# The gate product, the projection of p and the final norm with tokens as rows

## What is computed

```python
h = h + moe(rms_norm(h, norm2_g))           # top-4 of 32 experts, 12 MB of weights each
h = h + sigmoid(rms_norm(h, norm3_g) @ w_ple_gate) * (p @ w_ple_proj)
y = rms_norm(h, final_g)                    # w_ple_gate 1024x1024, w_ple_proj 256x1024
```

## Time and profile before

| | |
|---|---|
| median of three runs | 1280.57 us |
| the profiled execution: its time, its span | 1280.34 us, 1278.6 us |
| busy: PE, PEld, DVE, ACT | 1232.8, 675.9, 357.7, 225.9 us |
| loaded and stored | 455.84 MB, mean 357 GB/s |

### The profile page before, as it was taken

One profiled execution on the slowest core, in us unless ns is written; L12 is line 12 of the kernel. 1 busy time (PEld: TensorE's weight loads), 2 busy tenths in 40 slices (PEclk: granted clock), 3 DMA queues, 4 the chain that ended last, 5 costly groups with the idle time before them and its releaser, 6 DMA issues.

```text
span 1278.6 us, 15794 instructions
## 1 busy us (share of the span) xinstructions
PE 1232.8 (96%) x6210; PEld 675.9 (53%) x6210; DVE 357.7 (28%) x960; ACT 225.9 (18%) x432; POOL 22.6 (2%) x51
## 2 busy tenths in 40 slices
PE   8999999999999999999999999999999999999988
PEld 6886778886435434344443444444344443434446
DVE  3423633226222212122221212312122221212136
ACT  2322322013111111111111011111111111111123
POOL 2000110000000000000000000000000000000000
PEclk9999999999999999999999999999999999999999
DMA  9642586844899999999999999999999999999970
GB/s 295 211 132 67 174 272 225 334 165 173 345 429 427 427 427 429 429 429 428 430 427 429 427 427 423 429 427 427 428 429 429 428 429 429 428 429 428 427 280 34
DMA packets 71060, 455.84 MB, mean 357 GB/s; under 512 B 6622, under 2 KB 40972, under 8 KB 46436
## 3 DMA queue, kind: packets, MB, share of 16 engines
q1 hardware_dynamic: 65328, 443.83, 84.5%
q0 software_dynamic: 2608, 9.08, 2.1%
q10 hardware_dynamic: 3076, 2.27, 0.6%
HBM read 449.33 MB, written 5.83 MB: 356 GB/s over the span
## 4 chain that ended last, share of the span: by engine, by line
PE 76%; DMA 20%; DVE 3%; ACT 1%; issue 1%; POOL 0%; SPq 0%; DVEq 0%; ACTq 0%
PE bank L879 38%; PE bank L638 17%; DMA ring<-in_w_up_dram 13%; PE bank L895 5%; DMA ring<-in_w_gate_dram 5%; PE bank L914 4%; PE bank L939 3%; PE bank L1135 2%; PE bank L887 2%; DMA out_dram<-ring 1%; DMA ring<-in_w_in_dram 1%; DVE regC L1596 1%; DVE regC L1578 1%; PE bank L902 0%; PE bank L680 0%
## 5 line engine op out<-in xcount | busy, mean ns | idle before, releaser
L879 PE MATMUL bank<-ring,regC 128*64 128x512 f32 x2080 | 461.0, 597 | 21.4 <-DVE regC L1596 13.3
L879 PEld LDWEIGHTS bank<-ring,regC 128*64 128x64 f32 x2080 | 145.3, 137 | 298.7 <-issue 270.0
L1578 DVE TENSOR_TENSOR regC<-bank,biasT 128x512 f32<-128x512 f32 x62 | 42.9, 692 | 597.6 <-PE bank L887 596.1
L879 PE MATMUL bank<-ring,xe_odd 128*64 128x512 f32 x896 | 198.7, 594 | 7.7 <-DMA ring<-in_w_up_dram 6.6
L638 PE MATMUL bank<-regA,ring 128*128 128x264 f32 x832 | 194.3, 390 | 0.0
L638 PEld LDWEIGHTS bank<-regA,ring 128*128 128x128 f32 x832 | 156.4, 191 | 31.4 <-issue 3.8
L879 PEld LDWEIGHTS bank<-ring,xe_odd 128*64 128x64 f32 x896 | 62.8, 137 | 131.7 <-issue 116.8
L895 PEld LDWEIGHTS bank<-regC,regB 128*128 128x128 f32 x816 | 96.0, 192 | 13.8 <-issue 12.8
L895 PE MATMUL bank<-regC,regB 128*128 128x128 f32 x816 | 100.6, 277 | 0.3 <-ACT regE L1969 0.3
L2017 ACT ACTIVATE regD<-bank 128x512 f32<-128x512 f32 x62 | 37.0, 597 | 243.5 <-PE bank L879 243.5
L1603 DVE TENSOR_TENSOR hT<-hT,bank 128x264 f32<-128x264 f32 x144 | 56.8, 425 | 81.0 <-PE bank L914 28.0
(11 more groups left out here) (342 smaller groups left out, 665.9 us busy)
## 6 DMA issues: line engine op xcount, KB each, us to landing
ring<-in_w_up_dram SPq DMA_DIRECT2D x64, 2048.0 KB, 26.6
ring<-in_w_down_dram SPq DMA_DIRECT2D x64, 2048.0 KB, 28.4
ring<-in_w_gate_dram SPq DMA_DIRECT2D x64, 2048.0 KB, 23.5
ring<-in_w_in_dram SPq DMA_DIRECT2D x28, 1024.0 KB, 6.1
out_dram<-ring POOLq DMA_DIRECT2D x9, 512.0 KB, 5.1
ring<-in_state_gla_dram POOLq DMA_DIRECT2D x8, 512.0 KB, 5.1
ring<-in_w_o_dram SPq DMA_DIRECT2D x4, 1024.0 KB, 7.5
ring<-in_w_ple_gate_dram SPq DMA_DIRECT2D x2, 2048.0 KB, 34.6
```

The costliest lines, as they stand in the source:

```text
L879: ins = mm(bank[b][n * CAP:(n + 1) * CAP, :], lhs(k + i), by_k[s][:, i, n * 512:(n + 1) * 512], start=(k + i == 0), stop=(k + i == KT - 1))
L1578: return v.tensor_tensor(out, v_in, bias.to_broadcast([P, HALF, 2, CAP]), ALU.add)
```

## The change

The last stage works with tokens as rows. The 128 tokens of a block, as columns of `n3T`, stay in the array and 512 columns of W_ple_gate stream past: `gate_step(b, n)` for two blocks and two halves. The samples' gate is made on four column groups: the result has its 1024 features as 4 groups of 8 rows by 256 columns. h is turned to rows and stays in PSUM, from which ScalarE squares it (the accumulator gives the sums over features) and VectorE adds it. The reciprocal root goes into the sigmoid as its scale, one number for each row. The projection of p is made as rows too, in 7 units instead of 8 tiles: four for the tokens (512 columns for each block, then 384), one for columns 512 to 639 of both blocks, and two for the samples. final_g is loaded anew as rows, by five DMAs. At the end there are two stores for the tokens and four for the samples.

The diff shows the new lines of the parts named, and what is replaced only where it is short; bookkeeping of buffers and the last scaling are left out.

```diff
-        pwT = view(regE, 0, KT, T)
-        SWT = [view(regE, KT * T + i * T, T) for i in range(2)]
+        pw, pw_s = view(regE, 0, NB, D), view(regE, NB * D, 2 * P)
+        SWT = [view(regE, NB * D + 2 * P + i * T, T) for i in range(2)]
         logitsT = SWT[1]
...
+        gated, gated_s = view(regC, 0, NB, D), view(regC, NB * D, 2 * P)
+        fgrow, fgrow_s = view(regD, D, D), view(regD, 0, 2 * P)
...
-        ROUTER_BANK, ROW_BANKS, PW_BANKS = 3, ((4, 5), (6, 7), (0, 1)), (2, 4, 5, 6, 7, 2, 4, 5)
+        ROUTER_BANK, ROW_BANKS, PW_BANKS = 3, ((4, 5), (6, 7), (0, 1)), (2, 7, 4, 6, 2, 4, 5)
...
-        PW_EARLY, PW_RANKED = 3, 5
+        PW_TOKENS = {0: (0, slice(0, 512)), 2: (1, slice(0, 512)), 4: (0, slice(IN_GAP * P, D)), 5: (1, slice(IN_GAP * P, D))}
+        PW_SAMPLE = {1: ((0, 2, 4), (1, 3)), 6: ((6,), (5, 7))}
+        PW_EARLY, PW_RANKED, PW_UNITS = 2, 4, 7
...
-        GATE_BANKS, YROW_BANKS = (3, 0, 1, 2), ((4, 6), (7, 3), (0, 1))
+        GATE_BANKS, H2_BANKS, S_BANK, H2_SUM_BANK, Y_SUM_BANK = ((3, 0), (4, 3)), ((5, 6), (1, 2)), 7, 4, 0
+        S_HALVES = (slice(0, 2 * P), slice(2 * P, 4 * P))
...
-            sp.wait_ge(pw_done, IN_GAP)
+            sp.wait_ge(pw_done, PW_RANKED)
...
+            sp.wait_ge(h2_ready, KT)
+            sp.dma_start(fgrow, final_g.unsqueeze(0).to_broadcast([P, D])).then_inc(ld_final, 16)
+            for q in range(4):
+                sp.dma_start(fgrow_s[q * E:(q + 1) * E, :],
+                             final_g[q * 2 * P:(q + 1) * 2 * P].unsqueeze(0).to_broadcast([E, 2 * P])).then_inc(ld_final, 16)
+
+            for b, rows, t0 in BLOCKS[:NB]:
                 sp.wait_ge(yrow_ready["vector"], b + 1)
                 sp.wait_ge(yrow_ready["scalar"], b + 1)
-                dst = y_prompt[0, t0:t0 + rows, :] if b < NB else y_sample[:, 0, :]
-                sp.dma_start(dst, x2[0:rows, b, :]).then_inc(y_stored, 16)
-            sp.wait_ge(y_stored, 16 * len(BLOCKS))
+                sp.dma_start(y_prompt[0, t0:t0 + rows, :], x2[0:rows, b, :]).then_inc(y_stored, 16)
+            sp.wait_ge(yrow_ready["vector"], NB + 1)
+            for q in range(4):
+                sp.dma_start(y_sample[:, 0, q * 2 * P:(q + 1) * 2 * P], x2[q * E:q * E + NS, NB, 0:2 * P])\
+                    .then_inc(y_stored, 16)
+            sp.wait_ge(y_stored, 16 * (NB + 4))
...
+            def pw_rows(out, b, cols):
+                rows, t0 = BLOCKS[b][1:]
+                for k in range(PK):
+                    ins = mm(out, pTv[:, k, t0:t0 + rows], proj_cols(k, cols), start=(k == 0), stop=(k == PK - 1))
+                return ins
+
+            def pw_unit(n):
+
+                ps = bank[PW_BANKS[n]]
                 for b in range(NB):
-                    if PW_BANKS[f] in ROW_BANKS[b]:
+                    if PW_BANKS[n] in ROW_BANKS[b]:
                         pe.wait_ge(x2_ready, b + 1)
-                if PW_BANKS[f] in PW_BANKS[:f]:
-                    pe.wait_ge(pw_ready, PW_BANKS.index(PW_BANKS[f]) + 1)
-                for k in range(PK):
-                    w, at = (proj, f * P) if f < IN_GAP else (proj_rest, (f - IN_GAP) * P)
-                    ins = mm(bank[PW_BANKS[f]][:, 0:T], w[:, k, at:at + P], pTv[:, k, :],
-                             start=(k == 0), stop=(k == PK - 1))
+                if n in PW_TOKENS:
+                    b, cols = PW_TOKENS[n]
+                    ins = pw_rows(ps[:, 0:cols.stop - cols.start], b, cols)
+                elif n in PW_SAMPLE:
+                    for k, f in [(k, f) for blocks in PW_SAMPLE[n] for k in range(PK) for f in blocks]:
+                        q, at = f // 2, 2 * P + f % 2 * P
+                        ins = mm(ps[q * E:q * E + NS, at:at + P], pTv[:, k, L:T], proj_cols(k, slice(f * P, (f + 1) * P)),
+                                 start=(k == 0), stop=(k == PK - 1), skip_group_check=True)
+                else:
+                    for b in range(NB):
+                        ins = pw_rows(ps[:, b * P:(b + 1) * P], b, slice(512, IN_GAP * P))
                 ins.then_inc(pw_done, 1)
...
-            pe.wait_ge(pw_ready, PW_BANKS.index(GATHER_BANK) + 1)
...
-            pe.wait_ge(pw_ready, PW_BANKS.index(GATHER_BANK + 1) + 1)
+            pe.wait_ge(pw_ready, PW_RANKED)
...
+            in_quarters = [2 * q + j for j in range(2) for q in range(4)]
+            def gate_step(b, n):
+                s, t0 = (LAST + n) % SLOTS, BLOCKS[b][2]
                 for k in range(KT):
+                    if (b, n) == (0, 0):
                         pe.wait_ge(h2_ready, k + 1)
+                    if (b, n) == (0, 1) and k == HALF:
+                        sample_sums(H2_SUM_BANK, h2_squares, 1, h2_ss).then_inc(h2_s_sum, 1)
                     kf = LAST_ADDED[k]
+                    ins = mm(bank[GATE_BANKS[b][n]][:, :], n3T[:, kf, t0:t0 + P], by_col[s][:, kf, :],
                              start=(k == 0), stop=(k == KT - 1))
                 ins.then_inc(gate_done, 1)
 
+            def sample_sums(at, squares, count, ss):
+                pe.wait_ge(squares, count)
+                for q in range(4):
+                    ins = mm(bank[at][q * E:(q + 1) * E, 0:1], of_group[:, :], ss[:, 4:5], start=True, stop=True)
                 return ins
 
+            pe.wait_ge(slot_loaded[LAST % SLOTS], expert_loads(LAST))
+            gate_step(0, 0)
+            pe.wait_ge(s_clear, 1)
+            for f in in_quarters:
+                q, at = f // 2, 2 * P + f % 2 * P
+                ins = mm(bank[S_BANK][q * E:q * E + NS, at:at + P], hTv[:, f, L:T], ident[:, :], start=True, stop=True)
+            ins.then_inc(h2_turned, 1)
+            for b, rows, t0 in BLOCKS[:NB]:
+                for n in range(2):
+                    for j in range(HALF):
+                        ins = turn(bank[H2_BANKS[b][n]][:, j * P:(j + 1) * P], hTv[:, n * HALF + j, t0:t0 + P], ident[:, :])
+                    ins.then_inc(h2_turned, 1)
+            pe.wait_ge(slot_loaded[(LAST + 1) % SLOTS], expert_loads(LAST + 1))
+            gate_step(0, 1)
+            for k in range(KT):
+                for q in range(4):
+                    ins = mm(bank[S_BANK][q * E:q * E + NS, S_HALVES[0]], n3T[:, k, L:T],
+                             by_col[(LAST + q // 2) % SLOTS][:, k, S_HALVES[q % 2]], start=(k == 0), stop=(k == KT - 1),
+                             skip_group_check=True)
+            ins.then_inc(gate_done, 1)
+            pe.wait_ge(h2_sum, 1)
+            gate_step(1, 0)
+            pe.wait_ge(gate_act, 1)
+            gate_step(1, 1)
+            pe.wait_ge(gate_act, 2)
+            sample_sums(Y_SUM_BANK, y_squares, 3, y_ss).then_inc(y_s_sum, 1)
...
+            dve.wait_ge(extra.added, n_extra * KT + KT)
+            v.memset(bank[S_BANK][:, :], 0.0).then_inc(s_clear, 1)
+            dve.wait_ge(h2_s_sum, 1)
+            v.tensor_scalar(h2_rs[:, NB:NB + 1], bank[H2_SUM_BANK][:, 0:1], 1.0 / D, EPS, ALU.mult, ALU.add).then_inc(h2_sum, 1)
+            dve.wait_ge(h2_squares, 5)
+            link(v.tensor_tensor(h2_rs[:, 0:NB], h2_ss[:, 0:NB], h2_ss[:, NB:2 * NB], ALU.add))
+            v.tensor_scalar(h2_rs[:, 0:NB], h2_rs[:, 0:NB], 1.0 / D, EPS, ALU.mult, ALU.add).then_inc(h2_sum, 1)
+            dve.wait_ge(h2_root, 1)
+            v.reciprocal(h2_rs[:, :], h2_rs[:, :]).then_inc(h2_scale, 1)
+            dve.wait_ge(pw_ready, PW_UNITS)
+            dve.wait_ge(ld_final, 16 * 5)
+            for i, (g, p, h, final, out) in enumerate(
+                    [(gated[:, b, n * 512:(n + 1) * 512], pw[:, b, n * 512:(n + 1) * 512], bank[H2_BANKS[b][n]][:, :],
+                      fgrow[:, n * 512:(n + 1) * 512], x2[:, b, n * 512:(n + 1) * 512]) for b, n in ((0, 0), (0, 1))] +
+                    [(gated_s, pw_s, bank[S_BANK][:, S_HALVES[1]], fgrow_s, x2[:, NB, 0:2 * P])] +
+                    [(gated[:, b, n * 512:(n + 1) * 512], pw[:, b, n * 512:(n + 1) * 512], bank[H2_BANKS[b][n]][:, :],
+                      fgrow[:, n * 512:(n + 1) * 512], x2[:, b, n * 512:(n + 1) * 512]) for b, n in ((1, 0), (1, 1))]):
+                dve.wait_ge(gate_act, i + 1)
+                link(v.tensor_tensor(g, g, p, ALU.mult))
+                v.tensor_tensor(g, g, h, ALU.add).then_inc(h3_ready, 1)
+                dve.wait_ge(h3_ready, i + 1)
+                v.tensor_tensor(out, g, final, ALU.mult)
...
+            v.reciprocal(y_rs[:, :], y_rs[:, :]).then_inc(y_scale, 1)
             dve.wait_ge(y_scale, 1)
...
+            a(warm[:, 0:1], ones[:, 0:1], ACT.Sqrt)
             for n, f in enumerate(LAST_ADDED):
                 act.wait_ge(extra.added, n_extra * KT + (n + 1))
                 a(n3T[:, f, :], hTv[:, f, :], ACT.Copy, scale=vecT[:, 2 * KT + f:2 * KT + f + 1]).then_inc(h2_ready, 1)
+            act.wait_ge(h2_turned, 1)
+            a(x2[:, NB, 0:2 * P], bank[S_BANK][:, S_HALVES[1]], ACT.Square, accum_out=h2_ss[:, 4:5]).then_inc(h2_squares, 1)
+            for b in range(NB):
+                for n in range(2):
```

(75 more changed lines are left out.)

129 lines of the change are left out of this document (39 added, 90 removed).

## The result

The changed kernel takes 1283.8 us in the median of 8 executions, the kernel before beside it 1280.21 us: a ratio of 1.0033, 95% interval 1.0024 to 1.0042, or 4.2 us (3.1 to 5.4); the two medians themselves lie 3.6 us apart. The forecast was +6.1 us, 1286.4 us, in a range of 1283.2 to 1288.8.

The account below looks back on a forecast made before the run. TensorE's gate stage and tail bound the end, and loads after about 345 us follow the first pass. Projection +1.3, stage +5.4, tail -0.8, stores +0.2 make +6.1 on 1280.34: 1286.4 us, range 1283.2 to 1288.8.

Parts of the forecast that it names:

- Stage: Gate stage on TensorE at the kernel's end: 34.5 us against 29.14, so +5.4 us (bounds +4.5 and +6.0).
- excursion into the column groups: TensorE's change of product shape, in and out, for the samples' products: 0.3 us each (bounds 0.1 and 0.5).
- Tail: Hand-offs from the last gate product to the scaling of rows: 3.8 us against 4.60, -0.8 us (bounds -1.3 and 0).
- Front: Projection of p, around the selection and in the first expert's pass: +1.3 us, shifting later loads and the end.
- the work in the first pass: Projection of p inside the first expert's pass: 3.8 us in place of 2.94, so +0.9 us.
- The stores: Six store issues at the end, four for the samples in place of one: +0.2 us (bounds 0 and +0.9).
- Rival (2): TensorE's clock fall at 1225.7 us may not come once everything shifts by 1.3 us: 1284.7 us; chance 0.14.
- Rival (1): New turns and 8-column products in the gate stage bring on a half-clock stretch: 1288.1 us; chance 0.13.
- a sign of being wrong: A clock of 0.5 inside the gate stage, listed among the things that would show the forecast wrong.
- (3): The first pass's shift is made up by slack between loads and TensorE: 1285.1 us; chance 0.06.
- (4): Column groups in the samples' gate do not run at once: +10.4 us, 1296.8 us; chance 0.03.
- (5): Gate passes on TensorE are paced by weight load, not columns: 13.4 us less, 1273.0 us; chance 0.03.

Follow-up runs that it names:

- e7: The changed kernel with idle turns (14 and 20) added in the two waits of the last expert's pass; 1282.73 us, ratio 1.0030.
- e6: The kernel before with idle turns (14 and 20) added in the two waits of the last expert's pass; 1276.72 us, ratio 0.9976.
- e3: The kernel before with 12 idle turns of the identity added in the first expert's pass; 1280.03 us, ratio 1.0011.
- e8: The kernel before with its last three projection tiles moved to the 27th expert's pass, that loop round written out; 1276.11 us, ratio 0.9970.

## Why the prediction was right, and what it missed

**The terms held.** Stage +5.4 forecast, +5.1 measured: the 64 passes of 512 columns 28.1 us (27.8), samples 3.57 (3.8), turns 1.90 (1.8), samples' turns 0.55 (0.7), sums 0.17 (0.4). An excursion into the column groups cost some 0.1 us, not 0.3. Tail -0.8 forecast, -0.8 measured. Front +1.3 forecast, +1.2 to 1.5 measured, and carried to the end. Two of the terms are added up wrongly by 0.1, in opposite directions: the links of the tail, with the accumulator's 0.1, make 3.9 and not 3.8, and the work in the first pass makes 3.7 and not 3.8. The stores were mis-sized: +0.5 where 0.2 was taken, inside the bounds; the four issues of 0.56 us end 3.3 us behind the first store, and the span ends 2.0 us after the last. The sum is 6.0 to 6.3 against 6.1, and e7 against e6 shows it whole, within some 1.7 us.

**The step that failed** is the one that no term spoke of: the sum was made on an execution with a fall of the clock at 1225.7 us and kept that fall. Rival (2), the fall goes when everything shifts by 1.3 us, had 0.14 and 1284.7 us. By the mean clocks it is what happens in 11 of 15 executions. e3 shows that the shift alone is enough, and e6 and e7 that without falls the change costs its 6 us. So the median of 1283.8 us stands just below the 1284 that the terms reach at their bounds, and within the range because the range had been widened for rivals like this one; the profiled execution, 1286.21 us, lies at the forecast by luck, since its own fall of 6.8 us, 3.4 longer than the old one, made up for a start 1.6 us quicker. Rival (1), a fall in the new stage, took place in another form: 4 of 15 executions have a longer fall, but in both traces it begins at the last expert's waits and is over 6 us ahead of the new turns. It does reach into the stage's first 2 us, which the prediction had named as a sign of being wrong. The prediction also counts two falls in the trace of before; a third, from 1273.5 us to the end of the span, lies behind the last product and costs nothing.

**The others.** (3) is out by the table. (4) is out: 64 passes in 3.57 us are four at once. (5) is out: 0.436 us for 512 columns at full clock, where the Trainium skill's page "TensorE: Matmul & The Clock Gate" ("Back-to-back issue gap") has 131 ns at 512 columns, without a word on fp32; the measurement decides.

## What to carry to other kernels

Where a stage stands on one engine without a gap, counting passes by their spacing in like rows gave its time within 0.3 us of 34. Look at the granted clock of every profile before two of them are compared: a fall that follows a wait can move or vanish when anything ahead of it shifts, and here it was worth nearly a third of the change. A transfer queue that is busy throughout does not make each place on the other engine free: a place is cheap where that engine waits for transfers behind it (1.1 of 2.9 us were kept at the end), and not where it has fallen behind them. And look in the trace for a gain at the place that it was meant for: nearly two thirds of what e8's trace gained came from elsewhere.

## What was not expected of the hardware

- Idle products in two waits kept TensorE's clock at full, and the kernel before took 3.3 us less with them, 1.8 of it by the clock.
- The first 16 us differ by up to 2 us between executions of one kernel (the 17th pass of line L638 at 16.34 and 14.58 us), as the first passes are 0.44 or 0.22 us apart, and most of it stays to the end.
- At the branch behind the last expert TensorE waited 2.0 to 3.4 us without a releaser in ten traces, and a 16 KB packet on an instruction queue starts 2.6 to 2.7 us ahead of the wait's end; where the packet came 5.6 us or more ahead, the wait was not there.
